# A two-layer mixed-attention and mixture-of-experts step: norms and expert combinations taken tile by tile into the next projection

## The chip, the cores and the metric

The kernel runs on one core of one Trainium2 chip. The metric is device time in microseconds (us) of one launch. Lower is better.

## What is computed

Two groups of tokens go through two layers of width 1024: 512 prompt tokens and 32 sample tokens with a cache of 256 past positions. All data are fp32. Cut to what matters:

```python
for l in range(2):
    mod = silu(c) @ w_ada[l] + b_ada[l]              # shift, scale and gain rows of the layer
    sh1, sc1, g1, sh2, sc2, g2 = split(mod, 6)
    h = rmsnorm(x, norm_mix[l]) * (1 + sc1) + sh1
    # layer 0: projection to 3072 columns, 4 differential heads (rotary) and 8 stick-breaking heads
    # layer 1: projection to 3072 columns and 16 forget logits, 16 heads of forgetting attention
    x = x + g1 * (mixer(h) @ w_out)
    h = rmsnorm(x, norm_ffn[l]) * (1 + sc2) + sh2
    # 16 experts (1024 -> 512 gated -> 1024), each token goes to 2 of them
    x = x + g2 * moe(h)
y = rmsnorm(x, norm_final)
```

The new keys and values of both mixers and the log forget values are outputs too.

## The kernel before

**Tiles.** The 544 tokens are five row tiles: tiles 0 to 3 are the prompt (128 rows each), tile 4 (`NT`) is the 32 sample rows. `x` keeps them in SBUF throughout. `hT` and `hT2` hold the normed rows transposed.

**Split products.** fp32 products are made of three fp32r matmuls (`split_product`, lines 582 to 584). Each operand is split into a rounded high part (a copy on ScalarE: `fuse_high`, `split_high`) and the rest (a subtraction on VectorE, a quarter of it on GpSimd for the experts: `fuse_low`, `split_low`).

**Stages.** Each engine has its own hand-written instruction stream. Stages are parted by `phase_end` (line 176), where the engine drains, counts a semaphore up and waits for all of TensorE, ScalarE, VectorE and GpSimd. `PH` gives SyncE (SP), which issues most DMAs in program order, the value at which a stage is over. The order is setup, `ada0` (modulation rows), and for each layer `norm_mix`, `even` or `fox` (projection and attention), `out` (output projection and second norm), `route`, `moe`, `combine`; then `final`.

**First norm of a layer.** In `norm_mix` ScalarE sums squares and takes the root (`row_rstd`, in layer 0 already within `ada0`), VectorE multiplies by root and scale row (L509), GpSimd (tiles 0, 2, 4) or VectorE (1, 3) adds the shift row (L542, L514), TensorE transposes eight pieces of a tile (L562), ScalarE copies them to `hT` (L458) and VectorE writes the low part to `hT2` (L533). Before the scales, VectorE makes the scale rows ready once (L502).

**Projection.** `even_pe` and `fox_pe` work in 8 blocks of 384 columns (q, k and v of two heads) by 5 tiles. The products of block 0 come first; from then on each unit of attention of block i is woven with products of block i+1. Block 0's weights are split at the start of the stage (L631, L637). SP loads weights of block 1 (`fuse_load`, L622) when the phase before is over and block 0 is split. In layer 1 the forget logits (48 matmuls at the head of `fox_pe`) go first; from them ScalarE and VectorE make running sums (L1650 to L1667) that the first scores (L1439) need.

**Experts.** Tokens are sorted into items of up to 128 rows of one expert. An item has a gate, an up and a down product; its down product runs during the next item. Weight slabs `g`, `u`, `d` are in `ring` (low part), with high parts in `hT`, `work` and `arena`. SP loads the next slab when the product that used the buffer is done. After the loop the last item's down slab (L2128) waits for the down product of the item before. The scaled rows are scattered to DRAM by GpSimd (L1997) and SP reads them back per tile (L2168, L2172), tile 4 last.

**Combination.** VectorE adds the two expert rows (L2434), multiplies by the gain row (L2438, L2436) and adds to `x` (L2439); for tiles 1 and 3 GpSimd makes the last addition (L2421). Then all engines meet. After `combine0` comes `norm_mix1`; SP loads block 0's weights and the modulation rows of layer 1 when `moe0` is over. After `combine1` comes the final norm: `row_rstd`, scale (L2456), store (L2466).

## Time and profile before

| | us |
|---|---|
| median of 3 runs | 1777.8 |
| lowest and highest of them | 1762.39 and 1778.7 |
| span of the profiled execution | 1777.8 |
| TensorE matmul busy | 1496.0 (84%) |
| VectorE busy | 1027.2 (58%) |
| ScalarE busy | 863.7 (49%) |
| GpSimd busy | 498.2 (28%) |
| mean bandwidth to and from memory | 211 GB/s |

The profiled execution is one run, seen by the hardware profiler. Its span reaches from the first to the last instruction. Engines are called PE (TensorE), PEld (its weight loads), DVE (VectorE), ACT (ScalarE), POOL (GpSimd) and SP; a q behind a name is the engine's sequencer, which issues DMAs. L with a number is a line of the kernel. In a timeline a row is `start, duration, engine, line, operation, written<-read, count`, and in brackets how long the engine had stood before it and what released it. PEclk is TensorE's granted clock as a share of 2.4 GHz: 0.50 is the lower of its two levels, 1.2 GHz.

### The profile page before, as it was taken

The page shows a single profiled execution, that of the slowest core. Times are in us where ns is not written, and L with a number is a line of the kernel's source. Part 1 is how long each engine was busy: PE and PEld are TensorE (multiplying, and loading weights), DVE is VectorE, ACT ScalarE, POOL GpSimd, SP SyncE. Part 2 cuts the span into 40 slices and gives each one's busy share as a digit, 9 for nine tenths or more (in the row PEclk, how much of TensorE's full clock was granted, in tenths as well). Part 3 has the DMA queues.
Part 4 walks back from the last instruction along what each step waited for, and adds up shares of the span by engine and source line. Part 5 has one row for each costly group of instructions (what it writes and reads, how often), then busy time and mean ns, then how long its engine had stood idle before and what let it go on. Part 6 is the DMA issues. An engine that isn't in the chain of part 4 may idle for free. (4 is left out here: it accounts for less than half of the span.)

```text
span 1777.8 us, 22790 instructions
## 1 busy us (share of the span) xinstructions
PE 1496.0 (84%) x7971; PEld 1170.2 (66%) x7979; DVE 1027.2 (58%) x1341; ACT 863.7 (49%) x1512; POOL 498.2 (28%) x383
## 2 busy tenths in 40 slices
PE   3399999997947999999916999999889399999970
PEld 0387777764736877777715877777567277887760
DVE  0545532225455899899856433343363568889865
ACT  2233334445124877777614333343341268878751
POOL 1200111110104666566421000000001246666531
PEclk8699999998977999999956999999889599999985
DMA  8245553133044999899661333442421379999944
GB/s 282 74 159 188 177 183 102 67 127 102 1 192 155 380 350 347 341 360 347 264 239 50 97 102 102 130 145 97 155 71 63 140 287 374 368 368 370 351 188 173
DMA packets 148608, 358.62 MB, mean 202 GB/s; under 512 B 18660, under 2 KB 80868, under 8 KB 122420
## 3 DMA queue, kind: packets, MB, share of 16 engines
q1 hardware_dynamic: 136184, 333.25, 52.0%
q0 software_dynamic: 12352, 24.40, 3.7%
q8 instruction: 45, 0.74, 0.2%
q14 instruction: 27, 0.22, 0.0%
HBM read 341.87 MB, written 33.56 MB: 211 GB/s over the span
## 5 line engine op out<-in xcount | busy, mean ns | idle before, releaser
L583 PE MATMUL bank<-ring_r,arena_r 128*128 128x512 f32 x816 | 323.9, 397 | 0.0
L582 PE MATMUL bank<-ring_r,hT_r 128*128 128x384 f32 x640 | 238.7, 373 | 4.3 <-DVE ring_r L637 4.3
L584 PE MATMUL bank<-ring_r,work_r 128*128 128x384 f32 x640 | 216.9, 339 | 0.0
L583 PE MATMUL bank<-ring_r,hT_r 128*128 128x384 f32 x640 | 216.7, 339 | 0.0
L1905 DVE TENSOR_TENSOR ring_r<-ring,arena_r 128x1024 fp32r<-128x1024 f32 x102 | 169.5, 1698 | 40.3 <-ACT arena_r L1899 40.2
L1905 DVE TENSOR_TENSOR ring_r<-ring,work_r 128x1024 fp32r<-128x1024 f32 x102 | 175.0, 1741 | 28.6 <-ACT work_r L1899 28.5
L583 PEld LDWEIGHTS bank<-ring_r,arena_r 128*128 128x128 f32 x816 | 157.4, 193 | 31.3
L1905 DVE TENSOR_TENSOR ring_r<-ring,hT_r 128x1024 fp32r<-128x1024 f32 x102 | 145.9, 1458 | 25.0 <-ACT hT_r L1899 23.9
L1899 ACT ACTIVATE hT_r<-ring 128x1024 fp32r<-128x1024 f32 x136 | 136.2, 1054 | 37.7 <-DMA ring<-in_w_gate 37.7
L582 PEld LDWEIGHTS bank<-ring_r,hT_r 128*128 128x128 f32 x640 | 121.3, 190 | 45.5 <-issue 43.5
L1899 ACT ACTIVATE arena_r<-ring 128x1024 fp32r<-128x1024 f32 x136 | 134.6, 1051 | 27.4 <-DMA ring<-in_w_down 27.2
L1899 ACT ACTIVATE work_r<-ring 128x1024 fp32r<-128x1024 f32 x136 | 136.6, 1059 | 7.1 <-DMA ring<-in_w_up 7.0
L1858 POOL TENSOR_TENSOR arena<-arena,bc 128x1024 f32<-128x1024 f32 (+1 forms) x6 | 14.3, 2386 | 441.2 <-DVE arena L1844 441.2
L582 PE MATMUL bank<-arena_r 128*128 128x512 f32 x272 | 109.5, 402 | 19.6 <-DVE ring_r L1905 19.6
L583 PEld LDWEIGHTS bank<-ring_r,hT_r 128*128 128x128 f32 x640 | 121.7, 190 | 1.2 <-issue 0.7
L584 PEld LDWEIGHTS bank<-ring_r,work_r 128*128 128x128 f32 x640 | 121.0, 189 | 0.0
L2373 POOL TENSOR_TENSOR ring_r<-ring,arena_r 128x1024 fp32r<-128x1024 f32 x34 | 91.7, 2696 | 95.9 <-ACT arena_r L1899 95.9
L582 PE MATMUL bank<-hT_r,arena_r 128*128 128x512 f32 x272 | 114.5, 421 | 3.1 <-ACT arena_r L2262 3.0
L584 PE MATMUL bank<-hT_r,arena_r 128*128 128x512 f32 x272 | 110.8, 407 | 0.0
L582 PE MATMUL bank<-work_r,arena_r 128*128 128x512 f32 x272 | 109.2, 402 | 0.0
L680 ACT ACTIVATE arena<-bank 128x384 f32<-128x384 f32 (+1 forms) x48 | 23.4, 488 | 175.0 <-PE bank L584 175.0
L584 PE MATMUL bank<-arena_r 128*128 128x512 f32 x272 | 107.9, 397 | 0.0
(357 smaller groups left out, 2980.6 us busy)
## 6 DMA issues: line engine op xcount, KB each, us to landing
ring<-in_w_gate SPq DMA_DIRECT2D x68, 1024.0 KB, 6.9
ring<-in_w_up SPq DMA_DIRECT2D x68, 1024.0 KB, 7.3
ring<-in_w_down SPq DMA_DIRECT2D x68, 1024.0 KB, 7.2
bc<-in_w_ada SPq DMA_DIRECT2D x40, 1024.0 KB, 6.8
bc<-in_w_in_even SPq DMA_DIRECT2D x64, 192.0 KB, 3.9
bc<-in_w_in_odd SPq DMA_DIRECT2D x64, 192.0 KB, 3.5
ring<-in_w_ada SPq DMA_DIRECT2D x4, 2048.0 KB, 11.8
arena<-moe_out SPq DMA_DIRECT2D x8, 1024.0 KB
```

What stands on the lines that cost most here:

```text
L582: nc.tensor.matmul(acc, rows_hi, w_hi, start=first, stop=False)
L583: nc.tensor.matmul(acc, rows_hi, w_lo, start=False, stop=False)
L584: return nc.tensor.matmul(acc, rows_lo, w_hi, start=False, stop=last)
L680: act.activation(fu_rows[b % 2][0:rows(t), t, :], bank[n % 2][0:rows(t), 0:BW], ACT.Copy).then_inc(FU["ev_a"], 1)
L1858: pool.tensor_tensor(h_rows[0:r, t, :], h_rows[0:r, t, :], scale_shift(f"norm_ffn{l}", t)[1], ALU.add).then_inc(s["shifted"], 1)
L1899: act.activation(r32(piece(m_high[c], q)), piece(m_low[c], q), ACT.Copy).then_inc(MO[f"hi_{c}"], 1)
L1905: dve.tensor_tensor(r32(piece(m_low[c], q)), piece(m_low[c], q), f32(piece(m_high[c], q)), ALU.subtract).then_inc(MO[f"lo_{c}"], 1)
L2373: pool.tensor_tensor(r32(piece(m_low[c], 1)), piece(m_low[c], 1), f32(piece(m_high[c], 1)), ALU.subtract).then_inc(MO[f"lop_{c}"], 1)
```

## The change

- The stages `norm_mix` and `combine` and their meetings are taken out. Four meetings of all engines go: after the first norm of each layer and after each combination. That at the end of `moe` stays.
- Tiles are taken in the order 4, 0, 1, 2, 3 everywhere (`TILE_ORDER`), and the 32-row tile of expert results is read back first.
- Layer 0: ScalarE and VectorE split block 0's weights before the norm. TensorE's `lead_pe` transposes three tiles, then runs the products of block 0 with a tile of transposes after the first and the second. SP issues block 1's weights behind the modulation rows. The loads of the caches wait on GpSimd for its shifts.
- Layer 1: the same, with the combination of layer 0 (`combine`, all on VectorE now) woven tile by tile with scales, shifts and low parts, behind block 0's split. The forget logits move from the head to just before the fifth product; the chain of running sums follows later, and its transposes (`gate_rows`) from behind the third product to behind block 1's first.
- The last item's down weights go to the buffers of the gate slab. Their load waits for the last gate product and has semaphores of its own (`wl0`, `wl1`). ScalarE splits them before it copies out the results of the item before, VectorE and GpSimd likewise earlier.
- SP issues layer 1's block 0 weights and modulation rows (or `norm_final`) before it waits for the expert results.
- Final: VectorE weaves the five combinations with the five final scales; ScalarE's root of a tile waits for that tile's combination.

The core of the diff:

```diff
+        TILE_ORDER = (NT, 0, 1, 2, 3)
+        def row_turn(pe, l, j):
+            s, o, t = NORM, 2 * l, TILE_ORDER[j]
+            r = rows(t)
+            if j % 2 == 0:
+                pe.wait_ge(s["shifted"], 3 * o + j // 2 + 1)
+            else:
+                pe.wait_ge(s["shift_v"], 2 * o + j // 2 + 1)
+            if j >= 2:
+                row_evicted(pe, l, j - 2)
+            for half in range(2):
+                for k in range(4):
+                    d0 = P * (4 * half + k)
+                    last = nc.tensor.transpose(row_bank(j, half)[:, P * k:P * k + r], h_rows[0:r, t, d0:d0 + P], ident[0:r, 0:r])
+                last.then_inc(s["tr"], 1)
+
+        def lead_pe(pe, l, last_logits=None):
+            row_turn(pe, l, 0)
+            row_turn(pe, l, 1)
+            row_turn(pe, l, 2)
             for t in range(TILES):
+                row_evicted(pe, l, min(t + 1, TILES - 1))
+                if t == NT:
+                    pe.wait_ge(NORM["pad"], 2 * l + 2)
+                    if last_logits:
+                        last_logits()
+                fuse_product(pe, l, t, 0, KD)
+                if t + 3 < TILES:
+                    row_turn(pe, l, t + 3)
...
-            sp.wait_ge(g["phase"], PH["norm_mix0"])
             fuse_load(sp, 0, 1)
...
+            row_pool(pool, 0)
+            pool.wait_ge(NORM["gain"], 2)
             past(0)
             past(1)
...
-            sp.wait_ge(g["phase"], PH["norm_mix1"])
+            fuse_load(sp, 1, 1)
+            sp.wait_ge(NORM["shifted"], 9)
+            sp.wait_ge(NORM["shift_v"], 6)
             past(0)
             past(1)
-            fuse_load(sp, 1, 1)
...
-            for n in range(TILES):
-                fuse_product(pe, 1, n, 0, KD)
-                if n == 2:
-                    pe.wait_ge(FG["dve"], FG_DVE["logf"])
-                    for t in range(TILES):
-                        last = nc.tensor.transpose(bank[4][0:rows(t), N_FOX * t:N_FOX * t + N_FOX], fg_logf[:, cols(t)],
-                                                   ident[0:N_FOX, 0:N_FOX])
-                    last.then_inc(FG["pe"], 1)
+            lead_pe(pe, 1, gate_logits)
             fuse_product(pe, 1, TILES, 0, 2)
             turn_q_k(0)
             fuse_product(pe, 1, TILES, 2, 4)
             pe.wait_ge(FG["dve"], FG_DVE["biased"])
             turn_rest(0)
             fuse_product(pe, 1, TILES, 4, KD)
+            gate_rows()
             pe.wait_ge(FG["dve"], FG_DVE["first"])
             pe.wait_ge(FG["act"], FG_ACT["rows"])
             scores(0)
...
             for q in range(4):
                 fuse_low(dve, 1, 0, q)
+            row_gains(dve, 1)
+            combine(dve, 0, 0)
+            combine(dve, 0, 1)
+            row_scale(dve, 1, 0)
+            combine(dve, 0, 2)
+            row_scale(dve, 1, 1)
+            row_shift(dve, 1, 1)
+            row_low(dve, 1, 0)
+            combine(dve, 0, 3)
+            row_scale(dve, 1, 2)
+            row_low(dve, 1, 1)
+            combine(dve, 0, 4)
+            row_scale(dve, 1, 3)
+            row_shift(dve, 1, 3)
+            row_low(dve, 1, 2)
+            row_scale(dve, 1, 4)
+            row_low(dve, 1, 3)
+            fuse_rows_dve(dve, 1, 1)
+            row_low(dve, 1, 4)
+            fuse_low(dve, 1, 1, 0)
+            fuse_low(dve, 1, 1, 1)
+            fuse_rows_dve(dve, 1, 3)
             lk = Link(dve, FX["self_v"])
             dve.wait_ge(FG["pe"], FG_PE["logits"])
...
             dve.tensor_copy(fg_late[:, 0:PAST], bank[5][0:N_FOX, 0:PAST]).then_inc(FG["dve"], 1)
+            fuse_low(dve, 1, 1, 2)
+            fuse_low(dve, 1, 1, 3)
+            k_out(0)
             dve.wait_ge(FG["act"], FG_ACT["log"])
...
             e = expert(last)
+            sp.wait_ge(s["g"], last + 1)
+            load("d", e, last_down=True)
+            if l == 0:
+                fuse_load(sp, 1, 0)
             sp.wait_ge(s["d"], last)
-            load("d", e)
+            if l == 0:
+                mix_load(sp, 1)
+            else:
+                sp.dma_start(nf, a["norm_final"].partition_broadcast(P)).then_inc(AD["mix"], 16)
             sp.wait_ge(s["y"], 16 * end)
...
             split("d", last, 0, 1, 2, 3)
+            split_high(act, "d", last + 1, 0, 1, 2, 3, last_down=l)
             results_before(last, last_1)
             act_high_before(last + 1)
-            split("d", last + 1, 0, 1, 2, 3)
             results_before(last + 1, last)
...
             product(last)
+            split_low(dve, "d", last + 1, 0, 2, 3, last_down=True)
             act_low_before(last + 1)
-            split("d", last + 1, 0, 2, 3)
...
+        def combine(dve, l, j):
+            s, t = CO, TILE_ORDER[j]
+            r = rows(t)
+            y0, y1 = (v[0:r, :] for v in c_y[t])
+            lk = Link(dve, s["self"], base=2 * (TILES * l + j))
+            dve.wait_ge(s[f"y{t}"], 32 * (l + 1))
+            lk.do(dve.tensor_tensor(y0, y0, y1, ALU.add))
+            lk.do(dve.tensor_tensor(y0, y0, bc[0:r, G2, group(t), :], ALU.mult))
+            dve.tensor_tensor(x[0:r, t, :], x[0:r, t, :], y0, ALU.add).then_inc(s["acc"], 1)
...
         def final_dve(dve):
             dve.wait_ge(AD["mix"], 160 + 16)
-            for t in range(TILES):
+            combine(dve, 1, 0)
+            for j, t in enumerate(TILE_ORDER):
                 r = rows(t)
-                dve.wait_ge(NORM["rstd"], 4 * TILES + t + 1)
+                if j + 1 < TILES:
+                    combine(dve, 1, j + 1)
+                dve.wait_ge(NORM["rstd"], 4 * TILES + j + 1)
```

## Rows read from the trace of the kernel before

**Rows 1.** Windows: stretch, length, busy (count) of each engine, PEclk, DMA share, GB/s.

```profile
47.40:81.70 34.30, 8.26 (x40) 6.97 (x40) 20.36 (x21) 8.77 (x15) 10.62 (x9) 0.59 0.19 57
81.70:87.40 5.70, 5.63 (x18) 5.66 (x19) 2.66 (x4) 1.06 (x2) 1.17 (x2) 0.50 0.57 171
88.00:104.00 16.00, 16.00 (x93) 16.00 (x92) 6.07 (x12) 3.92 (x6) 0.00 (x0) 1.00 0.70 226
894.40:899.80 5.40, 5.31 (x13) 4.16 (x14) 2.39 (x3) 2.01 (x2) 2.27 (x1) 0.50 0.15 59
906.40:956.30 49.90, 8.69 (x40) 7.15 (x40) 39.12 (x32) 13.72 (x31) 13.92 (x8) 0.54 0.50 168
956.30:971.70 15.40, 15.29 (x48) 12.97 (x48) 3.57 (x5) 3.04 (x4) 0.77 (x1) 0.50 0.49 137
```

**Rows 2.** Timeline, first lead: start, us, engine, line, operation, count, idle, releaser.

```profile
57.84 2.35 DVE L502 SCALAR_TENSOR_TENSOR arena<-arena 128x1024 f32<-128x1024 f32 x2 [10.54 <-DMA arena<-in_norm_mix]
60.23 2.48 DVE L509 SCALAR_TENSOR_TENSOR arena<-x,rstd,arena 128x1024 f32<-128x1024 f32 x2
...
67.26 2.36 POOL L542 TENSOR_TENSOR arena<-arena 128x1024 f32<-128x1024 f32 x1 [2.36 <-DVE arena L509]
...
69.67 1.97 PE L562 MATMUL bank<-ident,arena 128*128 128x128 f32 x8 [0.98 <-POOL arena L542]
...
80.67 3.56 DVE L637 TENSOR_TENSOR ring_r<-bc,ring_r 128x768 fp32r<-128x768 f32 x4 [2.54 <-ACT ring_r L631]
...
81.77 0.66 PE L582 MATMUL bank<-ring_r,hT_r 128*128 128x384 f32 x1 [4.29 <-DVE ring_r L637]
```

**Rows 3.** Timeline, last item of layer 0 and what follows.

```profile
874.67 0.60 ACT L2268 ACTIVATE arena<-bank 128x512 f32<-128x512 f32 x1 [0.26 <-PE bank L584]
...
887.24 0.85 SPq L2128 DMA_DIRECT2D ring<-in_w_down  x2
...
889.09 0.69 DVE L2339 TENSOR_TENSOR arena_r<-bank,arena_r 128x512 fp32r<-128x512 f32 x1 [4.98 <-ACT arena_r L2272]
...
894.49 0.79 PE L582 MATMUL bank<-arena_r 128*128 128x512 f32 x1 [6.94 <-DVE ring_r L1905]
...
902.42 0.39 PE L584 MATMUL bank<-arena_r 128*128 128x512 f32 x1
...
905.41 1.00 POOL L1997 DMA_INDIRECT moe_out<-arena,now_out  x1 [0.86 <-POOL now_out L1994]
908.71 1.42 SPq L2168 DMA_DIRECT2D arena<-moe_out  x3
```

**Rows 4.** Timeline, combination and norm between the layers.

```profile
913.67 1.23 DVE L2434 TENSOR_TENSOR arena<-arena 128x1024 f32<-128x1024 f32 x1 [13.97 <-DMA arena<-moe_out]
...
919.97 3.17 POOL L2421 TENSOR_TENSOR x<-x,arena 128x1024 f32<-128x1024 f32 x1 [13.56 <-DVE arena L2436]
920.98 3.24 DVE L2438 TENSOR_TENSOR arena<-arena,bc 128x1024 f32<-128x1024 f32 x1
...
933.59 1.28 ACT L453 ACT_TABLE_LOAD   x1 [29.38 <-DVEq L178]
```

**Rows 5.** Timeline of DVE, forget gate.

```profile
975.38 0.71 DVE L1655 SCALAR_TENSOR_TENSOR arena<-arena 16x544 f32<-16x544 f32 x1 [2.11 <-ACT arena L1572]
...
980.44 0.98 DVE L1667 TENSOR_TENSOR arena<-arena,d_b 16x800 f32<-16x800 f32 x1
```

**Rows 6.** Timeline of PE, first scores of layer 1.

```profile
999.29 0.49 PE L1439 MATMUL bank<-arena 64*128 64x128 f32 x4
```

**Rows 7.** Timeline, the end.

```profile
1732.04 1.27 ACT L2280 ACTIVATE arena<-bank,slot_gate 128x512 f32<-128x512 f32 x2 [6.22 <-PE bank L584]
...
1737.79 2.09 SPq L2168 DMA_DIRECT2D arena<-moe_out  x4
...
1766.96 2.64 DVE L2456 SCALAR_TENSOR_TENSOR arena<-x,rstd,arena 128x1024 f32<-128x1024 f32 x2 [4.25 <-ACT rstd L482]
...
1773.73 0.33 SPq L2466 DMA_DIRECT2D out_y_sample<-arena  x1
```

More of the change, by code:

```diff
@@ L191, in encoder_step @@
         for l in range(2):
[L192 to L193 removed]
+            order += ([f"ada{l}"] if l == 0 else []) + ["even" if l == 0 else "fox"]
+            order += [f"out{l}", f"route{l}", f"moe{l}"]
         order += ["final"]
@@ L410, in ada_act @@
                     act.wait_ge(g["load_x"], 32)
-                    row_rstd(act, 0)
+                    for j in range(TILES):
+                        row_rstd(act, 0, j)
             act.wait_ge(g["load_rest"], 64)
@@ new lines, in row_shift, with row_bank, row_turned @@
+        def row_shift(dve, l, j):
+            s, o, t = NORM, 2 * l, TILE_ORDER[j]
+            dve.wait_ge(s["scaled"], TILES * o + j + 1)
+            dve.tensor_tensor(h_rows[:, t, :], h_rows[:, t, :], scale_shift(f"norm_mix{l}", t)[1], ALU.add).then_inc(s["shift_v"], 1)
+        def row_bank(j, half):
+            return bank[2 + (2 * j + half) % 4]
+        def row_turned(j, half):
+            return row_bank(j, half)[:, :].rearrange("p (k c) -> p k c", k=4)[:, :, 0:rows(TILE_ORDER[j])]
@@ new lines, in row_part, with row_high, row_low @@
+        def row_part(dst, j, half):
+            return dst[:, 4 * half:4 * half + 4, cols(TILE_ORDER[j])]
+        def row_high(act, l, j):
+            s, o = NORM, 2 * l
+            for half in range(2):
+                act.wait_ge(s["tr"], 10 * o + 2 * j + half + 1)
+                act.activation(r32(row_part(hT, j, half)), row_turned(j, half), ACT.Copy).then_inc(s["ev_a"], 1)
+        def row_low(dve, l, j):
+            s, o = NORM, 2 * l
+            for half in range(2):
+                dve.wait_ge(s["ev_a"], EV_A[o] + 2 * j + half + 1)
+                dve.tensor_tensor(r32(row_part(hT2, j, half)), row_turned(j, half), f32(row_part(hT, j, half)),
+                                  ALU.subtract).then_inc(s["ev_v"], 1)
@@ new lines, in row_turn @@
+        def row_turn(pe, l, j):
+            s, o, t = NORM, 2 * l, TILE_ORDER[j]
+            r = rows(t)
+            if j % 2 == 0:
[4 more added lines that the diff above has]
+                row_evicted(pe, l, j - 2)
+            for half in range(2):
+                for k in range(4):
+                    d0 = P * (4 * half + k)
+                    last = nc.tensor.transpose(row_bank(j, half)[:, P * k:P * k + r], h_rows[0:r, t, d0:d0 + P], ident[0:r, 0:r])
+                last.then_inc(s["tr"], 1)
@@ L1878, in encoder_step, with slab_of @@
         m_high = {"g": hT_flat[:, 0:SLAB], "u": work[:, 0:SLAB], "d": arena[:, 10240:10240 + SLAB]}
+        def slab_of(c, last_down):
+            return "g" if last_down else c
         def piece(v, q):
@@ L2447, in final_act @@
             act.preload_act_table_set("natural_log_exp_and_others")
-            row_rstd(act, 4)
+            for j in range(TILES):
+                row_rstd(act, 4, j, 1)
             phase_end("act", act)
```

320 lines of the change are left out of this document (126 added, 194 removed).

## Prediction

> **What bounds the kernel now.** I read the windows by stage first, then the timeline around each place where TensorE stands still. Inside a stage TensorE sets the time: from 88 to 104 us it is busy all of the time, and its 93 matmuls in 16 us give 0.172 us each (0.177 us for the 384-column ones of a projection, since transposes are among the 93) [rows 1]. Between stages it stands. From 47.4 to 81.7 us it works 8.3 us of 34.3, from 906.4 to 956.3 us 8.7 of 49.9 [rows 1], and it does nothing after 1732.0 [rows 7]. These three stretches are where the diff works; all else is moved as a block. Whatever starts the PE-bound stage earlier by some time ends it earlier by the same.
>
> In the first stretch VectorE waits 10.5 us for the modulation rows, norm and transposes follow, all engines meet, and only then are the first projection weights split, although VectorE was idle before [rows 2]. Between the layers the chain is: last down weights (issued 887.2, because they wait for the down product before), product until 902.8, rows out, rows back in (908.7), combination, meeting, table load, norm, transposes, meeting, gate logits [rows 3, 4]. At the end the same chain runs into the final norm [rows 7].
>
> **First lead.** The split of block 0 (3.56 us on VectorE, begun 0.95 us after ScalarE's) moves into VectorE's 10.5 us of waiting, its weights having been loaded before; it costs nothing as long as the rows land at 57.8, and up to 4.5 us if they came at once [rows 2]. SP issues block 1's 1.5 MB behind the modulation rows, which are in flight until 57.8; behind one another on one queue I price this 0, at worst 2 us. Then from 57.84: gains 2.35, scale and scale 2.48, a shift, a scale, POOL's shift to 69.6, the third transposes until 71.65, as before, since only the order of tiles differs [rows 2]. The low part of the second tile ends on VectorE near 72.7 (this replaces one 128-row subtraction by a 32-row one, and nothing else is ahead of it). TensorE's first product starts at 72.7 instead of 81.77 [rows 2], 9.1 us earlier. Two tiles of transposes now stand between products: 8 take 1.97 us at the low clock [rows 2], about 0.95 at the high one, so 1.9 us back. The clock: the products of 81.7 to 87.4 run at 1.2 GHz, those from 88 at 2.4 [rows 1]; I charge the new start the same 5.7 us (half of it is lost), before as after. Gain 7.2, and a little for a clock that has already risen during the transposes: 7.5 us. Bounds 5 and 10.
>
> **Last down weights (both layers).** The gate product of the last item is done at 874.6 (the silu follows it at 874.67) [rows 3]; the load now waits for that and not for the down product (887.2). Load to first product took 7.2 us [rows 3], so the weights could be used from 882, behind the transfer for the item before from about 884. VectorE is then the last: it is through with the item before at 884.1 (889.09 less the 4.98 it stood) [rows 3], and three subtractions of 1.23 us (the duration on a tensor of the same size [rows 4]) bring it to 887.8, with POOL in its way to 889. The activations' low part ends at 889.8 [rows 3]. The product starts there instead of 894.5: 4.7 us. The clock had fallen in the 7 us of standing (0.50 for 5.4 us [rows 1], 13 of 24 matmuls, 2.8 us lost). With only 2.3 us of standing it may hold: I take half, 1.4. Gain 6.1 per layer, bounds 2 and 7.5. SP also issues block 0 of layer 1 and its modulation rows here, 3.3 MB that were issued after 911; they run while TensorE computes, and only the rows out of the item before share the engines with them: 0, at worst 1 us.
>
> **Between the layers.** Now added up in order. The down product ends at 896.7; rows out are issued by 900.3 (906.4 less 6.1) and the remaining meeting is there; the rows come back in from 902.6 [rows 3]. ScalarE loads its table, 1.28 [rows 4], then splits; VectorE ends the four low parts 4.5 us later: 906.1. These were after the norm before; they now stand ahead of the combination, but 3.5 of it lie under the return of the rows, which land near 905. Gains: 2.35 to 908.5. A combination is three operations of 1.23, 3.7 us [rows 4]. Two of them: 915.8. Scale 917.1. Third: 3.7, and 2.0 for the collision with POOL's shift (below): 922.7. Scale, shift, low part of the 32 rows: 925.8. Fourth 929.5, scale 930.7, POOL's shift with a collision 3.2: 933.9, transposes 1.97: 935.9. The first product of layer 1 starts at 935.9 and not at 971.9, where it now stands behind 15.4 us of gate logits [rows 1]. VectorE's fifth combination, low parts and last scale end at 942, POOL's last shift at 944.4: before TensorE asks for them (transposes of the fourth tile 942.7, of the fifth 947.9). TensorE: first product 6.8 (5.6 us of it at 1.2 GHz), transposes 1, product 4.25, transposes 1, two products 8.5: 957.4. Gate logits: 15.4 us at the low clock [rows 1], at the high one half, 7.7: 965.1. Product 4.25: 969.3. A product and twelve transposes of q and k (as above 0.12 each): 5.7, so TensorE would be ready at 975.0. But the gate's chain is now behind: keys out at 972.0 come ahead of it on VectorE, then 5.06 us from the log values to the second part, 0.98 for the rest [rows 5], ScalarE's two copies 1.2 (an estimate, from VectorE's 0.98 for the same size): 979.3. In the kernel before this chain was under the products. TensorE waits 4.3 us, a new wait, and everything in the PE-bound stage with it. First scores 979.3 instead of 999.29 [rows 6]: gain 20.0, the 6.1 of the down weights in it. Bounds 12 and 26.
>
> The collision: VectorE's addition takes 1.23 alone and 3.24 beside POOL's, and POOL's takes 3.17 [rows 4] where alone it takes 2.36 [rows 2]. So each meeting of two such operations costs VectorE 2.0. By the Trainium skill, page "SBUF — State Buffer", section "SBUF: two separate sides", the loser of the shared port stands for the whole instruction of the other; by that a collision could cost 2.36, and the two here 0.7 us more in all. The row decides.
>
> **The end.** The product ends 6.0 us earlier than 1732.0; the rows come back from 1731.8 instead of 1737.79 [rows 7]. The first to come are now the 32 rows (two small transfers in place of 1 MB, whose data took 5.0 [rows 3, 4]): between 1 and 5, I take 2.6: 1734.4. Five combinations 18.5, with POOL out of them no collision, three scales of 1.28 between them: 1756.7. The root of the last tile (under it the fourth scale) is an estimate of 1.7: the 4.25 us before the first scale of the final norm hold the table load of 1.28 [rows 4] and two squares, one of them of the next tile, of about 1.2. Its scale 1.3: 1759.7. From the last store's issue to the end of the span there are 4.1 us (1773.73 to 1777.8) [rows 7]: 1763.8. The table load, the squares of four tiles and the meeting no longer stand behind the combinations. Gain 14.0, bounds 9 and 16.
>
> Sum: 7.5 + 20.0 + 14.0 = 41.5 us, 1777.8 − 41.5 = 1736.3. The profiled span equals the median of the runs shown, 1777.8.
>
> **Rivals.** (1) Gate logits and late clock. In 15.4 us with PE busy throughout, the logits of before never brought the high clock [rows 1]. Behind projections it may fall again: 7.7 us, and 1.4 us at each down product if the clock falls there too: 1747. Against it: products bring it within 5.7 us. Chance 0.2. (2) The last down weights bring nothing, since the queue, now also filled with layer 1's loads, or VectorE's splits deliver no sooner: 12 us, 1748. Against it: the weights are asked for 12.6 us earlier. 0.1. (3) Hidden anyway: the two leads start sooner, but block 1's weights, rotary work or the gate's chain hold TensorE later; only the end's 14.0 remain, 1764, within 1%. Speaks against it that each engine but TensorE has slack in 88 to 104 [rows 1]. 0.06. (4) Slower: in the new leads TensorE alternates transposes, waits and products, and the clock stays at 1.2 GHz far into the stage. Each us there loses 0.5; the gain is gone after 83 us of it, and after 140 us the time is 1806. Against it the 5.7 us. 0.03.
>
> **Numbers.** My forecast has 0.58, and 0.03 is left for more than 50 us of gain (clock held throughout, no gate wait). Faster by over 1% (what a measurement of this kernel can tell from no change) is 0.58 + 0.2 + 0.1 + 0.03 = 0.91, same 0.06, slower 0.03. The range reaches from 1736.3 less the clock's 2.8, the gate's 4.3 and the 9 us by which the bounds of the three sums could fall together, 1720, to rivals 1 and 2 together, 1757.
>
> **What would show it.** First product of layer 0 near 72.7 with block 0's splits before 57.8; load of the last down weights about 12 us ahead of the end of the down product, whose successor starts within 2.5 us; 30 to 36 us between the meeting after the experts and the first product; PEclk over the gate logits 1.0; an idle of about 4 us ahead of the first scores of layer 1; 32 to 34 us from the start of the rows' return to the end. Wrong would be: PEclk 0.5 beyond 10 us of dense products, a first VectorE wait on DMA in either lead longer than before, or the gate's wait above 8 us.

## The result, and the profile after

The changed kernel takes 1743.21 us (median of 4 runs, 1738.78 to 1750.45), the kernel before 1772.68 us (4 runs, 1762.39 to 1778.70). The ratio is 0.985, with a 95% interval of 0.981 to 0.989. It is faster, as forecast, but by 29.5 us and not by 41.5. A second measurement on another chip (e10 below) gives 1741.18 against 1769.95, ratio 0.981 (0.977 to 0.986).

I cut every profile at the same milestones, so that a row is the time since the milestone above it. A milestone is the start of the named work on TensorE, unless the row says that it ends. The kernel before was profiled three times in all (its first profile, e11, e12), the changed kernel twice (its first, e10). Because stages with heavy loads vary, the last two columns compare means, and what moved beyond the forecast is read from them.

| us since the milestone above | before, first | before, 3 profiles | after, first | after, second | gain of means | forecast |
|---|---|---|---|---|---|---|
| last modulation product | 45.21 | 45.2 to 46.8 | 46.22 | 46.44 | -0.3 | 0 |
| first projection product, layer 0 | 36.56 | 36.2 to 37.4 | 29.02 | 27.88 | 8.3 | 7.5 |
| output projection 0 | 348.01 | 347.5 to 348.1 | 347.86 | 347.58 | 0.2 | 0 |
| routing and expert items of layer 0 start | 109.95 | 109.1 to 110.0 | 109.62 | 109.70 | -0.1 | 0 |
| last transposes of activations, layer 0 | 347.18 | 338.1 to 347.2 | 347.50 | 350.20 | -6.6 | 0 |
| last down product starts | 7.58 | 7.6 | 3.53 | 3.54 | 4.1 | 4.7 |
| it ends | 8.32 | 7.4 to 8.3 | 7.36 | 7.08 | 0.7 | 1.4 |
| first projection product, layer 1 | 69.07 | 65.5 to 69.1 | 41.51 | 41.82 | 25.7 | 13.9 (both rows) |
| first scores, layer 1 | 27.41 | 27.4 | 42.67 | 42.39 | -15.1 | |
| output projection 1 | 304.16 | 300.0 to 304.2 | 308.53 | 310.41 | -7.4 | 0 |
| routing and expert items of layer 1 start | 111.18 | 110.6 to 111.2 | 111.18 | 109.88 | 0.5 | 0 |
| last transposes of activations, layer 1 | 301.13 | 298.7 to 301.1 | 305.58 | 304.56 | -4.9 | 0 |
| last down product starts | 7.53 | 7.5 to 7.7 | 3.39 | 3.31 | 4.3 | 4.7 |
| it ends | 8.60 | 7.5 to 8.6 | 5.76 | 5.78 | 2.3 | 1.4 |
| end of the span | 45.91 | 45.9 to 46.2 | 38.97 | 37.13 | 8.0 | 8.0 |

Outside the two rows of expert items the gain of the means is 31.0 us, 10.5 less than forecast. Those two rows are dealt with at e10 to e12.

The windows of the changed kernel (stretch, length, busy time and count of PE, PEld, DVE, ACT and POOL, PEclk, DMA share, GB/s):

```profile
48.40:75.20 26.80, 4.93 (x24) 4.06 (x24) 18.94 (x18) 7.45 (x12) 6.25 (x5) 0.55 0.66 206
75.20:80.00 4.80, 4.76 (x20) 4.79 (x21) 2.33 (x3) 0.00 (x0) 3.59 (x3) 0.69 0.01 3
883.70:887.00 3.30, 3.25 (x8) 2.58 (x9) 0.00 (x0) 0.00 (x0) 1.00 (x1) 0.51 0.99 284
887.00:891.20 4.20, 4.10 (x18) 3.03 (x16) 0.00 (x0) 0.00 (x0) 0.00 (x0) 0.98 0.49 176
898.50:932.60 34.10, 4.59 (x24) 4.09 (x25) 31.48 (x28) 13.11 (x26) 6.07 (x4) 0.50 0.49 174
952.00:961.00 9.00, 9.00 (x56) 7.94 (x54) 0.95 (x2) 0.00 (x0) 0.00 (x0) 1.00 0.00 0
975.00:985.00 10.00, 6.85 (x36) 5.45 (x36) 2.52 (x8) 2.88 (x11) 0.00 (x0) 0.83 0.77 211
985.00:995.00 10.00, 9.37 (x56) 6.84 (x60) 4.42 (x11) 3.10 (x11) 0.00 (x0) 0.83 0.58 216
1703.90:1709.80 5.90, 5.76 (x24) 4.42 (x24) 0.00 (x0) 0.00 (x0) 1.00 (x1) 1.00 0.13 51
```

The 34.3 us of the first lead [rows 1] are 26.8 now. The 49.9 us between the layers [rows 1] are 34.1, and VectorE works through 31.5 of them. The gate logits lie in 952 to 961, all at the high clock, where they took 15.3 us at the low one [rows 1].

The first lead in the timeline (start, us, engine, line, operation, count, idle before and what released it; in this and the following timelines rows are picked, and those between them are left out):

```profile
50.84 3.56 DVE L618 TENSOR_TENSOR ring_r<-bc,ring_r 128x768 fp32r<-128x768 f32 x4 [2.52 <-ACT ring_r L612]
...
59.85 2.35 DVE L465 SCALAR_TENSOR_TENSOR arena<-arena 128x1024 f32<-128x1024 f32 x2 [5.32 <-DMA arena<-in_norm_mix]
...
71.66 1.97 PE L526 MATMUL bank<-ident,arena 128*128 128x128 f32 x8 [1.65 <-POOL arena L511]
...
75.24 0.66 PE L563 MATMUL bank<-ring_r,hT_r 128*128 128x384 f32 x1 [1.62 <-ACT hT_r L494]
```

The split lies in VectorE's wait. The rows land 2.0 us later than before [rows 2], 1.0 of which the modulation products were late already, and the first product follows 15.4 us behind them, where 14.9 were forecast. All profiles with the new lead have these 15.4 us, and the old lead takes 23.9 to 24.4 in its four (the three of before, and e2). How long the rows take varies more, from 11.8 to 14.1 us behind the last modulation product with the new lead and from 11.9 to 13.3 with the old; whether block 1's load beside them costs some tenths of a us is open.

The last item of layer 0 and what follows it:

```profile
879.04 3.97 DVE L1945 TENSOR_TENSOR ring_r<-ring,hT_r 128x1024 fp32r<-128x1024 f32 x2 [0.52 <-ACT hT_r L1938]
882.94 0.68 DVE L2386 TENSOR_TENSOR arena_r<-bank,arena_r 128x512 fp32r<-128x512 f32 x1
883.75 0.79 PE L563 MATMUL bank<-hT_r,arena_r 128*128 128x512 f32 x1 [2.90 <-DVE arena_r L2386]
891.26 1.27 ACT L2327 ACTIVATE arena<-bank,slot_gate 128x512 f32<-128x512 f32 x2 [8.90 <-PE bank L565]
893.73 0.97 POOL L2037 DMA_INDIRECT moe_out<-arena,now_out  x1 [0.86 <-POOL now_out L2034]
897.17 0.33 SPq L2216 DMA_DIRECT2D arena<-moe_out  x1
898.50 1.28 ACT L1568 ACT_TABLE_LOAD   x1 [5.98 <-POOLq L178]
900.74 3.56 DVE L618 TENSOR_TENSOR ring_r<-bc,ring_r 128x768 fp32r<-128x768 f32 x4 [17.12 <-ACT ring_r L612]
906.60 1.21 DVE L2471 TENSOR_TENSOR arena<-arena,bc 32x1024 f32<-32x1024 f32 x1
915.23 3.25 POOL L511 TENSOR_TENSOR arena<-arena 32x1024 f32<-32x1024 f32 x1 [16.14 <-DVE arena L473]
916.31 3.25 DVE L2472 TENSOR_TENSOR arena<-arena,bc 128x1024 f32<-128x1024 f32 x1
928.60 2.35 POOL L511 TENSOR_TENSOR arena<-arena 128x1024 f32<-128x1024 f32 x1 [10.13 <-DVE arena L473]
932.62 0.67 PE L563 MATMUL bank<-ring_r,hT_r 128*128 128x384 f32 x1
```

TensorE no longer waits for the down weights themselves: it waits for the activations' low part, 2.9 us. But on VectorE this part comes straight behind the last two low parts of those weights (879.04), 0.6 us after ScalarE's copy is done (882.36), so a later split still delays it. POOL has issued its scatter at 894.70 (893.73 and 0.97), but ScalarE stands until 898.50 for POOL's sequencer. The whole lead is queued behind that moment, VectorE's splits first (idle 17.12).

The first scores of layer 1 and what stands behind them:

```profile
975.04 0.16 ACT L1599 ACTIVATE logf<-bank 32x16 f32<-32x16 f32 x1
975.22 0.38 SPq L1375 DMA_DIRECT2D out_fox_logf_p<-logf  x1
975.29 0.49 PE L1447 MATMUL bank<-arena 64*128 64x128 f32 x4 [4.21 <-ACT logf L1599]
978.24 4.15 SPq L603 DMA_DIRECT2D bc<-in_w_in_odd  x8
983.49 0.84 ACT L612 ACTIVATE ring_r<-bc 128x768 fp32r<-128x768 f32 x1 [6.24 <-DMA bc<-in_w_in_odd]
985.63 0.44 PE L1485 MATMUL bank<-arena 128*64 128x128 f32 x4 [3.49 <-ACT arena L1550]
```

The wait of 4.21 us ahead of the scores is the one forecast. Behind it is one that was not. SP stores the log forget values (975.22) and issues block 2's weights only then, 2.95 us after the first scores. In the first profile of the kernel before they went out ahead of the scores [rows 6], and ScalarE waited for them for 1.84 us:

```profile
985.41 0.38 SPq L1377 DMA_DIRECT2D out_fox_logf_p<-logf  x1
...
994.22 0.37 SPq L1367 DMA_DIRECT2D out_fox_k_p<-arena  x1
...
997.83 4.15 SPq L622 DMA_DIRECT2D bc<-in_w_in_odd  x8
...
1003.06 0.84 ACT L631 ACTIVATE ring_r<-bc 128x768 fp32r<-128x768 f32 x1 [1.84 <-DMA bc<-in_w_in_odd]
```

There the load went out behind the stores of block 0's keys and values (994.22), long after the log forget values. Here those stores are ready too and follow the log forget values without a gap: SP's release at 975.2 and the issue of six stores, 3.0 us, are what the load waits for.

The end:

```profile
1703.97 0.49 PE L563 MATMUL bank<-hT_r,arena_r 128*128 128x512 f32 x1 [2.75 <-DVE arena_r L2386]
...
1715.74 0.34 SPq L2216 DMA_DIRECT2D arena<-moe_out  x1
...
1718.80 1.21 DVE L2471 TENSOR_TENSOR arena<-arena,bc 32x1024 f32<-32x1024 f32 x1 [14.97 <-DMA bc<-moe_out]
...
1742.48 1.28 DVE L2493 SCALAR_TENSOR_TENSOR arena<-x,rstd,arena 128x1024 f32<-128x1024 f32 x1 [0.58 <-ACT rstd L457]
```

From the return of the rows to the end of the span it takes 33.0 us (1748.7 less 1715.74), where it took 40.0 (1777.8 less 1737.79 [rows 7]). VectorE starts 3.06 us behind SP (2.6 forecast), its last scale ends 24.96 us later (25.3 forecast), and 4.9 us are left for the last store (4.1 forecast).

### The profile page after: what moved, and what is told of

It is laid out like the page before. It is cut to its first block, busy times and chain, and to the rows that moved or that the text cites. A ratio compares the mean times of both kernels' runs of the same rounds, so it can differ in the third digit from the quotient of the medians.

```text
span 1748.7 us, 22798 instructions
## 1 busy us (share of the span) xinstructions
PE 1486.2 (85%) x7979; PEld 1162.0 (66%) x7979; DVE 1032.4 (59%) x1345; ACT 865.5 (49%) x1512; POOL 489.7 (28%) x379
## 4 chain that ended last, share of the span: by engine, by line
PE 65%; DVE 12%; issue 7%; ACT 6%; DMA 5%; SPq 2%; DVEq 1%; POOL 0%; POOLq 0%; ACTq 0%; PEldq 0%; PEld 0%
PE bank L563 17%; PE bank L565 15%; PE bank L564 15%; DVE ring_r L1945 4%; DMA ring<-in_w_gate 2%; PE bank L326 2%; ACT work_r L1938 2%; PE bank L1447 2%; PE bank L1485 1%; PE bank L676 1%; PE bank L332 1%; PE bank L1462 1%; PE bank L2231 1%; PE bank L919 1%; PE bank L558 1%
## 5 line engine op out<-in xcount | busy, mean ns | idle before, releaser
L1945 DVE TENSOR_TENSOR ring_r<-ring,hT_r 128x1024 fp32r<-128x1024 f32 x108 | 155.1, 1464 | 25.1 <-ACT hT_r L1938 24.3
L1938 ACT ACTIVATE hT_r<-ring 128x1024 fp32r<-128x1024 f32 x144 | 144.3, 1054 | 47.3 <-DMA ring<-in_w_gate 41.5
L1938 ACT ACTIVATE arena_r<-ring 128x1024 fp32r<-128x1024 f32 x128 | 126.8, 1052 | 21.6 <-DMA ring<-in_w_down 21.3
L563 PE MATMUL bank<-hT_r,arena_r 128*128 128x512 f32 x288 | 123.2, 428 | 8.9 <-DVE arena_r L2386 5.6
L565 PE MATMUL bank<-hT_r,arena_r 128*128 128x512 f32 x288 | 118.4, 411 | 0.0
L2421 POOL TENSOR_TENSOR ring_r<-ring,arena_r 128x1024 fp32r<-128x1024 f32 x32 | 86.3, 2696 | 90.9 <-ACT arena_r L1938 90.9
L563 PE MATMUL bank<-work_r,arena_r 128*128 128x512 f32 x272 | 109.2, 402 | 0.0
L2421 POOL TENSOR_TENSOR ring_r<-ring,hT_r 128x1024 fp32r<-128x1024 f32 x36 | 92.4, 2566 | 54.0 <-ACT hT_r L1938 40.4
L563 PE MATMUL bank<-arena_r 128*128 128x512 f32 x256 | 100.9, 394 | 6.7 <-DVE ring_r L1945 6.6
L565 PE MATMUL bank<-work_r,arena_r 128*128 128x512 f32 x272 | 106.4, 391 | 0.0
```

Source lines behind the costliest of these rows:

```text
L563: nc.tensor.matmul(acc, rows_hi, w_hi, start=first, stop=False)
L565: return nc.tensor.matmul(acc, rows_lo, w_hi, start=False, stop=last)
L1938: act.activation(r32(piece(m_high[v], q)), piece(m_low[v], q), ACT.Copy).then_inc(MO[f"hi_{c}"], 1)
L1945: dve.tensor_tensor(r32(piece(m_low[v], q)), piece(m_low[v], q), f32(piece(m_high[v], q)), ALU.subtract).then_inc(MO[f"lo_{c}"], 1)
L2421: pool.tensor_tensor(r32(piece(m_low[v], 1)), piece(m_low[v], 1), f32(piece(m_high[v], 1)), ALU.subtract).then_inc(MO[f"lop_{c}"], 1)
```

## The experiments

e1 to e4 ran on one chip (there the kernel before took 1769.97 us), e5 to e8 on a second (1772.09), e9 and e10 on a third (1769.95); e11 and e12 are single runs on a fourth. Each ratio is to the kernel before on the same chip.

### e1: the last down weights as before

```diff
-            return "g" if last_down else c
+            return c
...
-            sp.wait_ge(s["g"], last + 1)
+            sp.wait_ge(s["d"], last)
             load("d", e, last_down=True)
             if l == 0:
                 fuse_load(sp, 1, 0)
-            sp.wait_ge(s["d"], last)
+            sp.wait_ge(s["d"], last + 1)
```

ScalarE, VectorE and POOL split these weights behind the results of the item before, as in the kernel before.

> The changed kernel with only its last down weights put back: slab d of its own, load after the down product before, splits after the results and the activations. Theory (the gain of this part is carried in full at both layers): TensorE's last down product starts 3 to 4 us later behind the turn of the activations (7.5 us of standing instead of 3), and with the clock fallen it ends 5 us later in layer 0 and 7 us later in layer 1, so the whole is 10 to 14 us slower than the changed kernel. Rival (the weights were not what the end waited for): under 4 us slower.

Measured: 1758.82 us (10 runs), ratio 0.992 (0.989 to 0.995), 15.6 us above the changed kernel's first median, a little over the 10 to 14 expected. The down products start 8.0 and 7.6 us behind the transposes (3.5 and 3.3 in the changed kernel), which is 4.5 and 4.3, and their clock costs another 0.3 and 2.0. That makes 11.1 of the 12.1 us that I had put on both layers. The rest is in a place I had not looked at: from the down product's end to layer 1's first product it takes 45.5 us in place of 41.7. The timeline and the list of DMA issues (count, landing time of one) of this kernel:

```profile
887.02 1.75 SPq L348 DMA_DIRECT2D arena<-mod_rows  x4
889.59 1.00 POOL L2037 DMA_INDIRECT moe_out<-arena,now_out  x1 [0.86 <-POOL now_out L2034]
897.07 0.33 SPq L2216 DMA_DIRECT2D arena<-moe_out  x1
898.41 1.28 ACT L1568 ACT_TABLE_LOAD   x1 [10.02 <-POOLq L178]
```

```profile
moe_out<-arena,now_out POOLq DMA_INDIRECT x1, 7.3
```

The same list of the changed kernel:

```profile
moe_out<-arena,now_out POOLq DMA_INDIRECT x1, 3.3
```

In e1 SP issues the modulation rows of layer 1 at 887.02, and the last scatter travels beside them. e9 asks whether that is the cause.

### e9: only the modulation rows late

```diff
             load("d", e, last_down=True)
             if l == 0:
                 fuse_load(sp, 1, 0)
-            sp.wait_ge(s["d"], last)
+            sp.wait_ge(s["d"], last + 1)
             if l == 0:
                 mix_load(sp, 1)
```

> The changed kernel, except that SP issues the modulation rows and gains of layer 1 (and the final norm's gains in layer 1) behind the last down product instead of behind the one before it; the last down weights stay as early as in the changed kernel. Theory of contention: with only the last down weights undone, the last scatter took 7.3 us from issue to landing, beside these rows, where it takes 3.3 us in the changed kernel; if the rows are the cause and not the late weights, the down product still starts 3.5 us after the last transpose of activations (forecast: unchanged), the scatter takes about 7 us, and the time from the end of the down product of layer 0 to the first product of layer 1 goes from 41.5 to about 45.5 us; whole kernel 4 us slower than the changed one, about 1747 us. Rival: the late scatter came from the late weights or from POOL's order there; then this segment stays at 41.5 and the kernel at 1743 us.

Measured: 1746.13 us, ratio 0.987 (0.981 to 0.993), 5.0 us above e10 on the same chip. The segment to layer 1's first product is 46.8 us (41.7), and the list of DMA issues has

```profile
arena<-mod_rows SPq DMA_DIRECT2D x2, 512.0 KB, 4.6
...
moe_out<-arena,now_out POOLq DMA_INDIRECT x1, 8.5
```

So 0.5 MB of scatter takes 8.5 us beside these rows and 3.3 without them, and every engine waits for it. That is shown, since the edit moves nothing else in this layer, and from ScalarE's release to the first product it takes 34.1 us as in the changed kernel. By the Trainium skill, page "DMA: Bandwidth & Descriptors", section "SWDGE vs HWDGE vs iDMA", transfers issued by GpSimd and those issued by SyncE or ScalarE feed different queues in each DMA engine, which takes them in turns. This agrees with 3.3 against 8.5 us: the scatter isn't put ahead of rows issued before it. I had priced this traffic at "0, at worst 1 us". In the changed kernel the price is 0, but only because the rows are issued at 880.41 and have landed, at 890.3, before the last scatter starts. The scatter of the item before runs beside them there and takes 7.2 us, but it has landed too (891.1) before anything needs it.

### e2: the lead of layer 0 as before

```diff
-            order += ([f"ada{l}"] if l == 0 else []) + ["even" if l == 0 else "fox"]
+            order += ["ada0", "lead0", "even"] if l == 0 else ["fox"]
...
+            sp.wait_ge(g["phase"], PH["lead0"])
             fuse_load(sp, 0, 1)
```

All five tiles are normed and transposed, all engines meet, and then block 0 is split.

> The changed kernel with only the lead of layer 0 as before: all five tiles transposed, a meeting of all engines, then block 0's split and the products, block 1's load behind the meeting. Theory (an earlier start of a TensorE-bound stage is carried to its end): the first product starts 7 to 9 us later than in the changed kernel, the output projection of layer 0 also, and the total is 7 to 9 us longer. Rival (given back inside the stage): the first product is later but the output projection starts within 3 us of the changed kernel's.

Measured: 1750.88 us (9 runs), ratio 0.992 (0.988 to 0.995), 7.7 us above the changed kernel. The first product comes 37.8 us behind the last modulation product, 9.3 later than the mean of the changed kernel, and the 347.5 us to the output projection lie within the 347.3 to 349.2 of the other profiles. In this stage, then, what starts earlier does end earlier by the same.

### e5: the meeting without POOL's drain

```diff
             rows_out_before(last)
+            pool.sem_inc(g["phase"], 1)
             rows_out_before(last + 1)
-            phase_end("pool", pool)
+            phase_no["pool"] += 1
+            pool.wait_ge(g["phase"], 4 * phase_no["pool"])
```

POOL counts itself into the meeting before its last scatter, and does not drain behind it.

> The changed kernel, but GpSimd counts itself into the meeting at the end of the experts before it issues its last scatter of rows, and does not drain after it. Theory (in the changed kernel the meeting in layer 0 is over at about 898.4 us, 3.7 after GpSimd's issue ends, because its drain lasts until the scatter has landed, and everything of the woven lead stands behind it): ScalarE's table load comes within 1 us of its last result copy, 5 us earlier against TensorE's end, the rows' return is then what VectorE waits for, and the first product of layer 1 is 4 to 5.5 us earlier; total 4 to 5 us less. Rival (VectorE's combination is bound by the rows' return anyway): first product less than 1.5 us earlier.

Measured: 1736.18 us, ratio 0.979 (0.975 to 0.984). From the end of the down product to layer 1's first product it takes 35.7 us, 6.0 less. Its timeline:

```profile
887.13 1.28 ACT L1568 ACT_TABLE_LOAD   x1
888.23 0.97 POOL L2037 DMA_INDIRECT moe_out<-arena,now_out  x1 [0.86 <-POOL now_out L2034]
889.37 3.63 DVE L618 TENSOR_TENSOR ring_r<-bc,ring_r 128x768 fp32r<-128x768 f32 x4 [11.09 <-ACT ring_r L612]
895.30 1.21 DVE L2473 TENSOR_TENSOR arena<-arena,bc 32x1024 f32<-32x1024 f32 x1
```

ScalarE's table load stands straight behind its results, 1.5 us after the down product's end and not 7.4, and the splits run while the scatter is under way. The edit takes two things out of the way: the drain, 3.8 us in the changed kernel, and the last scatter's preparation and issue, about 2 us (892.69 to 894.70 there). Together they are the 5.9 us between 7.4 and 1.5. That the drain lasts as long as the scatter is seen in the nine profiles that have it in this place: ScalarE is released 1.5 us after the scatter's landing in each, whether the landing takes 3.3 us or, as in e1 and e9, 7.3 and 8.5. The expectation was 4 to 5.5 us; its further claim, that VectorE would then wait for the rows, did not come true, since it goes from the gain rows to the first combination without a stop (892.92 and 2.34, then 895.30). At the end of the kernel the same edit gains nothing (39.3 us, 37.1 to 39.7 in the changed kernel and its variants): there VectorE has nothing to do before the rows are back.

### e3, e4 and e7: the two waits around the first scores

e3 issues block 2's weights before SP's wait for the log forget values:

```diff
             past(1)
+            fuse_load(sp, 1, 2)
             sp.wait_ge(FG["act"], FG_ACT["rows"])
...
-                if i + 2 < NB:
+                if i >= 1 and i + 2 < NB:
                     fuse_load(sp, 1, i + 2)
```

e4 moves VectorE's copy of the new keys (`k_out(0)`) behind the gate's chain:

```diff
             fuse_low(dve, 1, 1, 3)
-            k_out(0)
             dve.wait_ge(FG["act"], FG_ACT["log"])
...
             dve.tensor_tensor(fg_res, fg_res, d2_b[0:N_FOX, :], ALU.subtract).then_inc(FG["dve"], 1)
+            k_out(0)
             dve.drain().then_inc(FG["dve"], 1)
```

e7 has both edits.

> The changed kernel, but SyncE issues layer 1's block 2 weights before it waits for the log forget rows and the stores of block 0. Theory (in the changed kernel ScalarE stands 6.2 us for these weights in the first unit of attention, TensorE 3.5 us for ScalarE, and the clock falls): both waits vanish and the time from first scores to output projection of layer 1, 308.5 us in the changed kernel and 304.2 before, returns to within 1 us of 304.5; total 3 to 5 us less. Rival (the stage lost its 4.4 us to the wait ahead of the first scores and the clock after it): it stays above 307.

> The changed kernel, but VectorE copies the keys of block 0 out after the forget gate's chain and not ahead of it. Theory (the chain waits 3.5 us behind the keys, which wait for TensorE's turn): the chain starts near 964 and not 967.6, TensorE's wait ahead of the first scores falls from 4.2 us to below 1.5, first scores 3 us earlier after the first product. Rival (the chain is bound by ScalarE's copies and the log rows, not by its start): first scores less than 1 us earlier.

> The changed kernel with both edits of the earlier runs: block 2's weights issued early, and keys copied out behind the forget gate's chain. Theory (two waits in a row; taking one away alone lengthens or bares the other: 5.1 us for weights in the run with keys late): first product to first scores 39.6 us, first scores to output projection 304 to 305.5, so 6 to 7 us less than the changed kernel over both. Rival (they overlap): under 4 us less.

| | median us | ratio (95%) | first product to scores | scores to output projection | both |
|---|---|---|---|---|---|
| before, mean of 3 profiles | | 1 | 27.4 | 302.0 | |
| changed, mean of 2 | 1743.2, 1741.2 | 0.985, 0.981 | 42.5 | 309.5 | 352.0 |
| e3, weights early | 1739.89 | 0.984 (0.978 to 0.990) | 43.0 | 305.4 | 348.5 |
| e4, keys late | 1740.85 | 0.984 (0.979 to 0.988) | 39.6 | 309.0 | 348.5 |
| e7, both | 1731.24 | 0.976 (0.971 to 0.981) | 39.4 | 301.9 | 341.3 |

TensorE's waits in e3 and in e4:

```profile
966.85 0.80 PE L1448 MATMUL bank<-arena 64*128 64x128 f32 x4 [4.20 <-ACT logf L1600]
```

```profile
964.02 0.49 PE L1447 MATMUL bank<-arena 64*128 64x128 f32 x4 [0.71 <-issue]
...
974.40 0.69 PE L1485 MATMUL bank<-arena 128*64 128x128 f32 x4 [5.05 <-ACT arena L1550]
```

Either edit alone leaves the other wait, and in e4 a part of the first wait's time comes back in the second, which grows from 3.49 to 5.05 us. Each of them gains 3.5 us over both segments, and e7 10.7, where 6 to 7 were expected. In e7 both are gone, and the stage behind the scores has the 302 us of the kernel before. The clock of e7:

```profile
961.00:971.00 10.00, 9.29 (x66) 8.07 (x65) 7.24 (x15) 5.98 (x17) 0.00 (x0) 1.00 0.71 194
971.00:981.00 10.00, 10.00 (x73) 7.12 (x71) 4.25 (x11) 3.02 (x10) 0.00 (x0) 1.00 0.61 212
```

It stays at 1.00, where it is 0.83 over 975 to 995 in the changed kernel. This accounts for the 10.7 us of e7 being more than the two waits of 4.21 and 3.49 (7.7 together): two windows of 10 us at 0.83 lose about 3.4 us, for the low clock comes behind each of the two waits, from about 976 to 979 and from 986 to 989.5, while TensorE is busy. The eight profiles that have the weights late (two of the changed kernel, e1, e2, e4, e5, e6 and e9) all take 307.6 to 310.5 us from scores to output projection, e7 and e8 301.9.

### e6: the combinations first, then the norm

```diff
-            combine(dve, 0, 0)
-            combine(dve, 0, 1)
+            for j in range(TILES):
+                combine(dve, 0, j)
             row_scale(dve, 1, 0)
-            combine(dve, 0, 2)
...
-            combine(dve, 0, 3)
...
-            combine(dve, 0, 4)
```

> The changed kernel with VectorE's order in the lead of layer 1 unwoven: all five combinations first, then scales, shifts and low parts; meetings stay out. Theory (the lead is bound by VectorE's chain, so what stands ahead of the third tile's shift counts): first product of layer 1 3 to 5 us later than in the changed kernel, of the 27.6 us by which the change shortened this stretch; most of it comes from meetings, load times and the splits moved, not from weaving. Rival (weaving is what gives the gain): over 8 us later.

Measured: 1750.16 us, ratio 0.986 (0.980 to 0.993). The segment to the first product is 46.9 us, 5.2 more than in the changed kernel. So of the 25.7 us that this segment lost, about 5 are due to the weaving itself. The gate logits, which stand behind the first product now, were 15.5 us of it (956.4 to 971.9 before). The rest I put down to the splits under the rows' return and to the meetings; no run takes these apart.

### e8: e5 and e7 together

> All three edits on the changed kernel: block 2's weights early, keys late, GpSimd early into the meeting. Theory (independent places): 10 to 12 us less than the changed kernel, 1731 to 1733 us; 6 to 7 us of it between first product and output projection of layer 1 and 4 to 5 ahead of the first product. Rival: under 6 us less in all, since the expert stages vary by more than that from run to run.

Measured: 1725.03 us (6 runs, 1722.58 to 1739.69), ratio 0.973 (0.969 to 0.977). The segments are 36.0, 40.1 and 301.9 us: each gain is kept, 16.2 to 18.2 us in the medians where 10 to 12 were expected from parts of 4 to 5 and 6 to 7; the parts turned out to be 6.0 and 10.7. This kernel beats both others, the one before by about 47 us.

### e10, e11 and e12: the kernels again, unaltered

> The changed kernel once more, nothing altered, for the variation of the expert stages. Theory: the 305.6 us of the expert items of layer 1 in its first profile (301.1 before) are variation of the stage between executions; a second profile would show something between 299.5 and 304, the rest of the segments within 1 us of the first profile (first product to scores 42.7, scores to output projection 308.5, the end 39.0). Rival: the change itself makes these items slower by 4 us; then 305 or more again. Time about 1743 us by either.

> The kernel before once more, nothing altered, for its expert stages: its only profile so far shows 347.2 us for the items of layer 0 and 301.1 us for those of layer 1 (together 648.3), where the changed kernel showed 653.1 and 654.8 and its variants 637.9 to 654.6. Theory of variation: the kernel before moves over a like range from one profile to the next, so this one may be anywhere between 638 and 655. Rival, the change makes the items about 4 us slower: the kernel before stays at or below 648 in this and the next profile. The segments outside the items within 1 us of its first profile.

> A third profile of the kernel before, for the same question. If one of the two shows more than 650 us for the items of both layers together, variation alone can give the 4.8 us between the first two profiles; if both lie at or below 648, the rival stands undecided, and the document says so.

e10's items of layer 1 take 304.6 us, between what the two sides expected; of its other segments, four lie more than the expected 1 us off the first profile (1.1 to 1.9). For both layers together the changed kernel has 653.1 and 654.8 us, the kernel before 648.3, 640.2 and 638.8. By what I had written, the second and third profile of before leave the rival undecided. The other kernels say more: e2 to e9 have the changed kernel's expert items unaltered, and seven of these eight take 637.9 to 646.5 us for them, e8 654.6. The changed kernel's two profiles are also its longest runs, 1750.45 and 1749.44 us, with the other six at 1735.5 to 1743.4. So the items take their short time in kernels with the change too, and I take the 11.5 us between the means of the profiles for variation between executions. That is argued from these numbers and not shown, and why an execution has the long or the short items is open.

The three profiles of before also correct a reading of mine. Its first one has 304.2 us for the stage behind the scores, the others 300.0 and 302.0. The loss there is 7.4 us by means, where the two first profiles give 4.4.

## Why the prediction was right and where it was wrong

**Right: the first lead.** Forecast 7.5, measured 8.3 between means. The products ran at the low clock for 3.0 us and not for 5.7 (PEclk 0.69 over the 4.8 us from 75.2), so rival 4, in which the clock stays low far into the stage, has nothing to stand on.

**Right: the end.** Forecast 14.0 with the down weights, measured 14.6.

**Right: the wait ahead of the scores and the clock of the gate logits.** Forecast 4.3 and measured 4.21 us; forecast 1.0 and measured 1.00. Rival 1 is refuted in its main part, the 7.7 us for the logits at the low clock. Its other part, the clock at the down products, came true in layer 0.

**Mis-sized: the last down weights.** The term was 6.1 and 6.0 us; means give 4.8 in layer 0 and 6.6 in layer 1. The starts are 4.1 and 4.3 us earlier for 4.7, since TensorE stands 2.9 us and not 2.3. The half of the clock that I had given to each layer is no half in fact: in layer 0 it fell (0.51, then 0.98), in layer 1 it held (1.00 over 1703.9 to 1709.8). That layer 1 came out above the term is luck. The ten profiles with this part of the change (all but before's and e1) have 20 such products: in 7 of them TensorE stood 4.0 to 4.4 us and in the other 13 it stood 2.4 to 2.9, in 5 the clock held, and by the mean of all 20 the part gives 4.6 us per layer (3.7 at the start, 0.9 in the product). Rival 2 is wrong, as e1 shows.

**Wrong step 1: "rows out are issued by 900.3 ... and the remaining meeting is there".** I let the meeting end with POOL's issue of the scatter. It ends when POOL has drained, and that was 3.8 us behind the issue (894.70 to 898.50), 1.3 us behind SP's own release by the landed scatter (897.17). With "VectorE ends the four low parts 4.5 us later" all of the lead moved by it. In this profile the meeting came 7.4 us behind the down product's end (891.1), with 3.6 forecast. Of these 3.8 us some were made good, such as POOL's shift at 928.60, which took 2.35 us where I had charged 3.2: from the down product's end to the first scores the means have 84.2 us, the forecast had 82.6. That is 1.6 us. Another 1.7 us lie in the kernel before, whose first profile took 96.5 us there, its three 94.8. Together they are the 3.3 us between 13.9 and 10.6 (25.7 less 15.1). e5, in which neither the drain nor the last issue holds the meeting, gains 6.0 us; 3.8 of them are the drain.

**Wrong step 2: "Whatever starts the PE-bound stage earlier by some time ends it earlier by the same."** It holds in layer 0 (e2). In layer 1 it fails by 7.4 us, on top of the wait ahead of the scores, which had been counted. The argument followed the gate chain to its first reader, TensorE, and stopped. The log forget values have a second reader, SP, which stores them, and behind that store in SP's queue stand the weights of block 2. The chain was under other work before, and the load waited for block 0's stores of keys and values; once the chain became what the scores wait for, the load came 3 us behind the scores rather than 1.5 ahead of them. e3, e4 and e7 show it. I had named what the new wait holds up on TensorE and what stands ahead of the chain on VectorE, but nothing on SP. Rival 3, in which the gate's chain holds TensorE later, had this mechanism in part but priced it as the loss of both leads.

**The sum.** 41.5 less 3.3 (the drain, and the longer first profile of before), less 7.4 (block 2), less 1.3 and plus 0.6 (down weights), plus 0.8 (first lead), and 0.1 for the small rows and rounding is 31.0 us. The medians give 29.5 and 28.8, within their intervals of that.

**The collision** of VectorE and POOL went as forecast: 3.25 us beside POOL's addition, 1.23 alone. VectorE's instruction at 916.31 ends 1.08 us behind POOL's (918.48). Of the two collisions that the prediction charged, the second did not lengthen POOL's shift (2.35 us at 928.60); it was VectorE's addition beside it (929.64) that took 2.39 us for 1.23, and nothing on the path stood behind it. By the Trainium skill, page "SBUF — State Buffer", section "SBUF: two separate sides", the loser stands for the whole instruction of the other, and the trace agrees with it here.

## What to carry to other kernels

When a producer moves onto the critical path, follow every reader of it, the DMA queue first: a small store that waits for it holds back each load issued behind it. Where an engine drains behind a scatter ahead of a meeting, the meeting costs the scatter's way to memory and not its issue alone; if work that does not need the scattered rows stands behind the meeting, let the engine count itself in before the scatter, provided that the readers have a semaphore of their own. And before a stage is charged with a few us, profile both kernels more than once.

## What the runs showed of the hardware

- A GpSimd drain behind an indirect scatter of 0.5 MB held the meeting until 1.5 us after the scatter's landing in all nine profiles that have it between the layers. Alone, the scatter landed 3.3 us after the start of its issue, and the meeting was over 3.8 us after the issue's end. Beside modulation rows and gains that had been issued before it, the landing took 7.3 us (e1, DMA share 0.88 meanwhile) and 8.5 us (e9, 0.72).
- After equal gaps the clock fell or held. In the 13 last down products that started 3.0 to 3.5 us behind the start of the transposes, it held in 5 (5.76 to 5.78 us for 24 matmuls) and fell in 8 (7.1 to 8.6 us). I found nothing in the profiles that tells the two apart. In the 15 that started 4.6 to 8.0 us behind it, it fell every time (7.1 to 8.6 us).
- Over the 14 profiles the expert items of both layers take 638 to 655 us, 2.6%, and 639 to 648 in three profiles of one program, while the 348 us from the first product to layer 0's output projection stay within 0.6%.
